# Router products on x times its scale, the root applied per token, router and memory-gate products in four column tiles

## What is computed

```python
def rmsnorm(x, g):
    y = x * lax.rsqrt(jnp.mean(x * x, axis=-1, keepdims=True) + EPS)
    return y * g

def latent_layer(x, mods, ...):
    sh1, sc1, g1, sh2, sc2, g2 = mods
    h = rmsnorm(x, ln1_g) * (1 + sc1) + sh1
    (cb, cc, ch), (nq, nk, nv), (mq, mk, mv), mo, ig, fg = project(h, w_in, ml_gate_b)
    ...
    x = x + g1 * merge(conv_o, na_o, ml_o, w_out)
    h2 = rmsnorm(x, ln2_g) * (1 + sc2) + sh2
    x = x + g2 * hier_moe(h2, w_rg, b_rg, w_re, b_re, w_gate, w_up, w_down)

def hier_moe(h, ...):
    gl = x @ w_rg + b_rg                  # 4 groups, x is h2
    el = (x @ w_re + b_re)                # 16 experts
    # best group, two best experts in it, softmax weights
    # expert: silu(x @ w_gate) * (x @ w_up), then @ w_down
```

## Time and profile before

| | |
|---|---|
| time, median of 3 runs | 1158.72 us (1154.29 to 1158.77) |
| profiled execution | 1159.24 us, span 1157.4 us |
| TensorE products (PE) | 1083.0 us busy, 94% |
| weight loads of TensorE (PEld) | 594.0 us, 51% |
| VectorE (DVE) | 396.9 us, 34% |
| ScalarE (ACT) | 246.0 us, 21% |
| GpSimd (POOL) | 56.5 us, 5% |
| mean granted clock of TensorE | 0.979 of full speed |
| read from HBM | 298.34 MB |

### The profile page before, as it was taken

How to read it: one execution, slowest core, us unless ns; L and a number is a source line. 1 busy time by engine, 2 the same in 40 slices (tenths; PEclk the granted TensorE clock), 3 DMA queues, 4 the chain that set the end, 5 groups by cost and what they waited for, 6 DMA issues and landing times.

```text
span 1157.4 us, 15554 instructions
## 1 busy us (share of the span) xinstructions
PE 1083.0 (94%) x6146; PEld 594.0 (51%) x6146; DVE 396.9 (34%) x1144; ACT 246.0 (21%) x517; POOL 56.5 (5%) x82
## 2 busy tenths in 40 slices
PE   3999999989999999999989999998898999999995
PEld 2546655676555445544334564566554644355443
DVE  3503033166282223222352301417627212222334
ACT  2210113152132111111141001415213211011113
POOL 1221000000002000000020000000000000000002
PEclk8999999999999999999999999999898999999998
DMA  8967562289618999999952445426450799999981
GB/s 312 362 169 217 192 219 84 74 312 308 271 36 311 401 412 412 413 413 413 405 201 73 146 155 211 153 74 255 128 217 2 294 360 413 412 398 406 414 353 55
DMA packets 92764, 302.59 MB, mean 261 GB/s; under 512 B 5789, under 2 KB 6161, under 8 KB 84369
## 3 DMA queue, kind: packets, MB, share of 16 engines
q1 hardware_dynamic: 89104, 293.84, 66.5%
q0 software_dynamic: 3584, 7.71, 2.8%
HBM read 298.34 MB, written 4.99 MB: 262 GB/s over the span
## 4 chain that ended last, share of the span: by engine, by line
PE 84%; DVE 6%; DMA 4%; ACT 2%; issue 2%; POOL 1%; SPq 0%; DVEq 0%; POOLq 0%; ACTq 0%
PE ps L1436 18%; PE ps L1005 17%; PE ps L1015 9%; PE ps L1492 9%; PE ps L1190 7%; PE ps L1257 5%; PE ps L959 4%; DMA ring<-in_w_up 3%; PE ps L1285 2%; PE ps L949 2%; PE ps L1287 2%; PE ps L1221 1%; PE ps L995 1%; PE ps L1155 1%; DMA ring<-in_w_mod 1%
## 5 line engine op out<-in xcount | busy, mean ns | idle before, releaser
L1005 PE MATMUL ps<-ring,hT 128*128 128x512 f32 (+1 forms) x480 | 194.9, 565 | 0.0
L1436 PE MATMUL ps<-ring,arena 128*64 128x512 f32 x608 | 174.4, 598 | 3.3 <-DMA ring<-in_w_up 3.3
L1005 PEld LDWEIGHTS ps<-ring,hT 128*128 128x128 f32 x480 | 90.5, 190 | 98.0 <-issue 94.7
L1436 PE MATMUL ps<-slot,arena 128*64 128x512 f32 x352 | 137.5, 601 | 2.0 <-issue 2.0
L2146 DVE SCALAR_TENSOR_TENSOR xT<-ps,modT,xT 128x128 f32<-128x128 f32 (+1 forms) x288 | 97.3, 409 | 69.4 <-PE ps L1190 60.2
L1015 PE MATMUL ps<-hT,ring 128*128 128x384 f32 x320 | 105.3, 487 | 0.0
L1436 PEld LDWEIGHTS ps<-ring,arena 128*64 128x64 f32 x608 | 54.9, 138 | 90.6 <-issue 90.6
L1190 PE MATMUL ps<-mixT,ring 128*128 128x384 f32 x256 | 85.1, 494 | 1.9 <-ACT mixT L1728 1.9
L1015 PEld LDWEIGHTS ps<-hT,ring 128*128 128x128 f32 x320 | 60.2, 190 | 41.5 <-issue 1.8
L2379 DVE TENSOR_TENSOR hT<-ps,arena 128x512 f32<-128x512 f32 x16 | 11.1, 692 | 203.6 <-PE ps L1436 203.6
L1492 PE MATMUL ps<-slot,arena 128*64 128x512 f32 x208 | 72.0, 597 | 0.0
(11 more groups left out here) (357 smaller groups left out, 1264.4 us busy)
## 6 DMA issues: line engine op xcount, KB each, us to landing
ring<-in_w_mod SPq DMA_DIRECT2D x24, 2048.0 KB, 12.5
ring<-in_w_gate SPq DMA_DIRECT2D x38, 1024.0 KB, 12.8
ring<-in_w_up SPq DMA_DIRECT2D x38, 1024.0 KB, 10.4
ring<-in_w_down SPq DMA_DIRECT2D x32, 1024.0 KB, 13.4
ring<-in_w_in SPq DMA_DIRECT2D x14, 2048.0 KB, 12.0
slot<-in_w_down SPq DMA_DIRECT2D x26, 1024.0 KB, 12.9
slot<-in_w_gate SPq DMA_DIRECT2D x22, 1024.0 KB, 11.4
slot<-in_w_up SPq DMA_DIRECT2D x22, 1024.0 KB, 10.6
```

What stands on the lines that cost most here:

```text
L1005: mm = pe.matmul(p[:, 0:n], hT[:, k, t * P:(t + 1) * P], w[:, k, c0:c0 + n], start=(k == 0), stop=(k == KT - 1))
L1436: mm = pe.matmul(out[which][64 * s:64 * s + 64, :], xg[:, k, cols[s]], w[i][:, k % 4, :], start=(k == 0), stop=(k == KT - 1))
```

## The change

**Router stage.** The router no longer works on normed tiles. With root r per token, gain a and shift b per feature, h2 = (x a) / r + b. ScalarE writes x a for tiles 0 to 6 into `hT` under the output products, VectorE for tile 7. TensorE multiplies these by `wroute`, now padded to 32 columns; tile k goes to column tile k mod 4 of the array, on partitions 32 (k mod 4) onward, so the eight products leave four partial sums (`parts`). Three products with a stacked identity add them and turn them to token order. The mean of squares is also made in token order (six products with one output column a tile, L1299), its root and reciprocal are three columns, `token_rstd`, and VectorE multiplies the logits by it and adds a bias that has the product of shift and router weights in it (`shift_bias`). That product comes from VectorE (two multiplications and a reduction) and one TensorE product, which stands ahead of the head transposes. For h2 the 24 transposes of x a stay open in PSUM, and six products of 512 columns add r b: the row of roots `std` times a diagonal of shifts that GpSimd builds (`shift_diag`). ScalarE and VectorE multiply by `token_rstd` as they drain h2. The squares move from `hT` to the space of `zqk`, and the banks of this stage are given one by one.

The core of the diff:

```diff
-    steps = [("gates",)]
-    steps += [("by_token", "mq", t) for t in range(3)] + [("by_token", "mk", t) for t in range(3)]
+    steps = [("gate_parts",), ("by_token", "mq", 0), ("gates",)]
+    steps += [("by_token", "mq", t) for t in (1, 2)] + [("by_token", "mk", t) for t in range(3)]
...
+                for j in range(2):
+                    pool.tensor_tensor(shift_diag[:, j], ident[:, None, :].broadcast_to((P, KT, P)),
+                                       modT[:, d, 24:32, j, None].broadcast_to((P, KT, P)), ALU.mult
+                                       ).then_inc(ly.shifts_ready, 1)
...
-                def gates():
+                def gate_sums():
                     pe.wait_ge(ly.wgp_ready, ly.number + 1)
-                    p = begin("gates")
+                    p = begin("gate_parts")
                     keep_busy(p, 5)
                     for k in range(KT):
                         wait_normed(0, k)
-                        mm = pe.matmul(p[:, 0:NT], wgp[:, k, :], hT[:, k, :], start=(k == 0), stop=(k == KT - 1))
-                    done(mm, "gates")
+                        lanes = slice(32 * (k % 4), 32 * (k % 4) + 32)
+                        mm = pe.matmul(p[lanes, 0:NT], wgp[:, k, :], hT[:, k, :], start=(k < 4), stop=(k >= 4))
+                    done(mm, "gate_parts")
+
+                def gates():
+                    bk.wait_drained(pe, "gate_parts")
+                    p = begin("gates")
+                    done(pe.matmul(p[:, 0:NT], cst[:, C_GATES:C_GATES + P], gate_parts, start=True, stop=True), "gates")
...
+                pe.wait_ge(ly.shift_sum_ready, ly.number + 1)
+                done(pe.matmul(begin("shift_logits")[:, 0:40], ones, shift_sum, start=True, stop=True), "shift_logits")
                 for h in range(4):
                     pe.wait_ge(ly.hnorm_ready, 4 * ly.number + h + 1)
...
-                sum_squares(1)
-                p = begin("lgT")
-                keep_busy(p, 5)
-                for k in range(KT):
-                    wait_normed(1, k)
-                    mm = pe.matmul(p[0:20, 0:NT], wroute[:, k, :], hT[:, k, :], start=(k == 0), stop=(k == KT - 1))
+                begin("lgT")
+                for k in range(4):
+                    route(k)
+                for k in range(4):
+                    turn_gained(k)
+                for k in range(4, KT):
+                    mm = route(k)
                 done(mm, "lgT")
+                sums = begin("sums")
+                for t in range(TILES):
+                    for k in (0, KT - 1):
+                        mm = pe.matmul(sums[:, t:t + 1], squares[1][:, k, t * P:(t + 1) * P], mean[:, 0:1],
+                                       start=(k == 0), stop=(k == KT - 1))
+                done(mm, "sums")
                 bk.wait_drained(pe, "lgT")
                 p = begin("lg")
                 for t in range(TILES):
-                    mm = pe.transpose(p[:, t * 20:(t + 1) * 20], lgT[:, t * P:(t + 1) * P], ident[0:20, 0:20])
+                    mm = pe.matmul(p[:, t * 20:(t + 1) * 20], parts[:, t * P:(t + 1) * P], cst[:, C_PARTS:C_PARTS + 20],
+                                   start=True, stop=True)
                 done(mm, "lg")
+                sum_squares(1)
+                for k in range(4, KT - 1):
+                    turn_gained(k)
+                turn_gained(KT - 1)
+                bk.wait_drained(pe, ("ss", 1))
+                pe.wait_ge(ly.shifts_ready, 2 * ly.number + 2)
                 for i in range(6):
-                    for n in range(4):
-                        mm = pe.transpose(p[:, n * P:(n + 1) * P], hT[:, upper * 4 + n, t * P:(t + 1) * P], ident)
+                    done(pe.matmul(ps[bk.bank(("h2", i))][:, :], std[:, t * P:(t + 1) * P],
+                                   shift_diag[:, 0 if t == 0 else 1, upper * 4:upper * 4 + 4, :].rearrange("p k n -> p (k n)"),
+                                   start=False, stop=True, skip_group_check=True), ("h2", i))
...
+                def gain():
+                    for k in range(KT):
+                        bk.wait_drained(act, ("wo", k))
+                        act.activation(squares[1][:, k, :], xT[:, k, :], ACT.Square).then_inc(ly.squares_ready, 1)
+                        if k < KT - 1:
+                            for j, cols in STREAMS:
+                                ins = act.activation(hT[:, k, cols], xT[:, k, cols], ACT.Copy, scale=gains[:, L, 1, k, j:j + 1])
+                            ins.then_inc(ly.gained_act, 1)
+                    p = full_of("lgT")
+                    drain("lgT", act.copy(parts, p[:, 0:NT]))
+                    p = full_of("sums")
+                    drain("sums", act.activation(token_root, p[:, 0:3], ACT.Sqrt, bias=eps))
+                    p = full_of(("ss", 1))
+                    drain(("ss", 1), act.activation(std[:], p[:, 0:NT], ACT.Sqrt, bias=eps))
...
+                for j in range(2):
+                    ins = dve.tensor_tensor(shift_route[:, j], wroute[:, :, 0:20], modT[:, L, 24:32, j, None].broadcast_to((P, KT, 20)),
+                                            ALU.mult)
+                link(ins)
+                dve.tensor_reduce(shift_sum.rearrange("p (j n) -> p j n", j=2), shift_route.rearrange("p j k n -> p j n k"),
+                                  AX.X, ALU.add).then_inc(ly.shift_sum_ready, 1)
...
-                drain("lg", dve.tensor_tensor(logits, p[:, 0:60].rearrange("p (t n) -> p t n", t=3),
-                                              rbias[:, None, :].broadcast_to((P, 3, 20)), ALU.add))
+                drain("lg", dve.tensor_tensor(logits, p[:, 0:60].rearrange("p (t n) -> p t n", t=3), wide(token_rstd, 20),
+                                              ALU.mult))
                 bk.wait_drained(dve, "lg")
+                link(dve.tensor_tensor(logits, logits, shift_bias, ALU.add))
```

More of the change, by code:

```diff
@@ L157, in constant_table @@
     t[:, C_JOB:C_JOB + OVERFLOW] = np.arange(OVERFLOW) + 0.5
+    for part in range(4):
+        for c in range(16):
+            t[32 * part + c, C_GATES + 32 * (c // 4) + c % 4] = 1.0
+    for part in range(4):
+        t[32 * part:32 * part + 20, C_PARTS:C_PARTS + 20] = np.eye(20)
     t[:, C_EPS] = EPS
@@ L226, in place_products @@
     for kind, *args in mixing_steps(layer):
-        if kind == "gates":
-            spread("gates")
+        if kind == "gate_parts":
+            spread("gate_parts")
+        elif kind == "gates":
+            spread("gates", over=before_heads)
         elif kind == "by_token":
@@ L263, in place_products @@
             bk.place(("C", *args), 7)
-    spread(*[("wo", m) for m in range(EARLY_OUT)], *[("hT", h) for h in range(4)],
-           *[("wo", m) for m in range(EARLY_OUT, 8)], ("ss", 1))
-    spread("lgT", "lg", *[("h2", i) for i in range(6)], "rank")
+    for m in range(EARLY_OUT):
+        bk.place(("wo", m), m)
+    bk.place("shift_logits", 5)
+    for h in range(4):
+        bk.place(("hT", h), HEAD_BANKS[h])
+    for m in range(EARLY_OUT, 8):
+        bk.place(("wo", m), m % 3)
+    bk.place("lgT", 7)
+    bk.place("sums", 1)
+    bk.place("lg", 7)
+    bk.place(("ss", 1), 5)
+    for i in range(6):
+        bk.place(("h2", i), H2_BANKS[i])
+    bk.place("rank", 5)
     for x in range(2):
@@ L607, in build @@
         loop_selw = sel[:, :, P:2 * P]
-        lgT = arena[0:20, 0:NT]
-        squares = (mixT, hT)
+        shift_diag = arena[:, 0:2048].rearrange("p (j k n) -> p j k n", j=2, k=KT)
+        shift_route = arena[:, 2048:2368].rearrange("p (j k n) -> p j k n", j=2, k=KT)
+        shift_sum = arena[:, 2368:2408]
+        shift_bias = arena[:, 2408:2468].rearrange("p (t n) -> p t n", t=3)
+        parts = arena[:, 2496:2496 + NT]
+        token_root = small[:, 48:51]
+        token_rstd = small[:, 52:55]
+        squares = (mixT, zqk[:].rearrange("p t d -> p (t d)").rearrange("p (k n) -> p k n", k=KT))
         xrow = ring[:, RING - 1, 0:3072].rearrange("p (t d) -> p t d", t=3)
@@ L976, in sum_squares @@
                     p = begin(("ss", n))
-                    if n == 1 or not ly.first:
-                        keep_busy(p, 2 if n == 1 else 4)
+                    if n == 0 and not ly.first:
+                        keep_busy(p, 4)
                     pe.wait_ge(ly.summed_ready, (n + 1) * (KT - 2))
@@ L1208, in _, with wait_gained, route, turn_gained @@
                     bk.wait_drained(pe, ("hT", h))
+                def wait_gained(k):
+                    if k < KT - 1:
+                        pe.wait_ge(ly.gained_act, ly.number * (KT - 1) + k + 1)
+                    else:
+                        pe.wait_ge(ly.gained_dve, ly.number + 1)
+                def route(k):
+                    wait_gained(k)
+                    lanes = slice(32 * (k % 4), 32 * (k % 4) + 32)
+                    return pe.matmul(ps[bk.bank("lgT")][lanes, 0:NT], wroute[:, k, :], hT[:, k, :], start=(k < 4),
+                                     stop=(k >= 4))
```

(27 more changed lines are left out.)

95 lines of the change are left out of this document (61 added, 34 removed).

## The result

The changed kernel takes 1149.58 us, the median of six runs (1147.39 to 1154.96), against 1158.63 for the kernel before in the same series. The ratio over all runs is 0.9933, with a 95% interval of 0.9907 to 0.9959; the two medians alone would give 0.9922. By the medians the gain is 9.05 us where 20.2 were forecast, and the time lies outside the range of 1132 to 1148. The profiled execution took 1154.96 us (span 1153.2, mean granted clock 0.975) and is the slowest of its six. The time goes with that clock: 1147.39 us came at 0.983. So I compare stages of the profiled executions, not their whole spans.

A forecast was written before the change was run, and what follows sets the result against it. TensorE bounds nearly everywhere, with engines waiting on each other in the router stage and experts living on their weight stream. 18.4 + 3.1 - 1.05 - 0.25 = 20.2 us off 1159.24 gives 1139.0, median 1138.6; range 1132 to 1148.

The forecast's parts named there:

- part 1: Router stage moved onto TensorE: 7.9 us won in layer 0 and 10.5 in layer 1, 18.4 us, if TensorE never waits.
- At most by half: VectorE's heads ahead of the output products: if GpSimd's diagonals disturbed them, their 3.24 us would grow by 1.6 us a layer.
- the filler's rows: Trace rows of six filler pieces in the router stage: 4.51 and 5.46 us after the clock fell, 2.6 at full clock.
- Router stage: From last output product to first expert product: 24.3 us in each layer, against 32.2 and 34.8 before.
- the rank row: Trace row of the router stage's rank products, 0.126 us a piece, used to price the one-column sum pieces at 1.5 us.
- Gates: Gate products on four column tiles side by side: 3.1 us won in layer 0, 0 in layer 1.
- New wait ahead of the heads: TensorE needs the shift sum before the head transposes: 0.8 us stall, -1.05 in all in layer 0; -0.25 in layer 1.
- Stream: Expert weight loads are not held and move with TensorE; the wait for the last weights stays near 19 us.
- The sign that I gave, 11 us earlier: Expert stage of layer 0: the wait for the last weights, still near 19 us, comes 11 us earlier.
- column tiles that do not overlap: Rival: 3.8 us more in each router stage and 3.8 in layer 0's gates, 1150 us; chance 0.04.
- The clock rival: Rival: clock falls earlier in the router stage, costing 2 to 3 us a layer, 1143 to 1149, say 1144; chance 0.13.
- the chance of 0.03 for a cost not seen: Whole kernel: an unforeseen cost leaves the time within 0.5% of the kernel before; chance 0.03.

The follow-up runs named there:

- experiment 1: The changed kernel, with GpSimd's two multiplications for the diagonals held until VectorE has made the shift sum; 1135.29 us, ratio 0.9802 against the kernel before.
- experiment 7: experiment 4 with the gate products of the kernel before the change, router stage as changed; 1139.83 us, ratio 0.9838 against the kernel before.
- experiment 4: experiment 1 with VectorE's shift sum made before its last heads and GpSimd starting behind the fourth head's norm; 1134.53 us, ratio 0.9785 against the kernel before.
- experiment 5: experiment 4 without the four filler pieces ahead of the ranks and with two instead of six behind them; 1130.55 us, ratio 0.9755 against the kernel before.

## Why the prediction was wrong

**The step that failed** is the one on the diagonals in part 1: "GpSimd builds the diagonals after its stores of the memory state, ahead of the 33.78 us of output products, which cover them; if they disturbed VectorE, the heads' 3.24 us would grow, at most by half, 1.6 us a layer." Three things in it are wrong.
- The work does not meet the heads' 3.24 us, it meets one of the three operations before them. I had asked where the result is used (far behind, after the output products), not what VectorE does when GpSimd starts. The trace of before has GpSimd's stores there, so the place could be read.
- It is a hold, not a slowing. "At most by half" was a guess without a row. The hold is 4.9 us (5.75 - 0.88), longer than the 3.77 us of the two GpSimd operations that the trace shows beside it.
- Its cost is not covered, because the new wait for the shift sum, which I priced at 1.05 us, puts the end of all VectorE work directly ahead of TensorE. TensorE's idle time of 5.6 us then costs clock. By the profiled executions of experiment 1 and the changed kernel the whole is 9.1 us in layer 0 and 8.2 in layer 1. By the medians it is 14.3 us for both layers; the changed kernel's profiled execution is 5.4 us above its median.

I should have carried it as a rival: GpSimd's work holds VectorE for its whole length. A price from this kernel's rows was to be had, since VectorE had 0.35 us to spare ahead of the heads in layer 0 and 2.4 in layer 1, and a fall of the clock costs 2 to 3 us by the filler's rows.

**The steps that held.**
- Router stage: 24.25 us in both layers against 24.3. The pieces fit one by one: 16 route pieces 1.56 (1.4), 24 transposes 2.77 (2.8), twelve one-column pieces 1.43 (1.5), twelve shift pieces 5.15 (5.1). Pricing the one-column pieces by the rank row was right: they took 0.12 us each.
- Gates: 2.9 us in layer 0 against 3.1; in layer 1 a loss of 0.4 by experiment 7 against 0.
- New wait ahead of the heads: 0.75 us idle in layer 0 (forecast 0.8) and none in layer 1, in experiment 1, where nothing holds VectorE. With the product it costs 11.3 - 10.1 = 1.2 us (forecast 1.05).
- Stream: the wait for the last weights of layer 0 is still 18.66 us long (18.92 before). It moved with TensorE, and no second round of experts ran. In the changed kernel it begins at 541.67, later than before (540.54); in experiment 1 at 530.92, 9.6 us earlier. The sign that I gave, 11 us earlier, did not follow from my own sum, which makes 7.9 + 3.1 - 1.05 = 9.95.
- Column tiles overlap, as the earlier trace rows said: eight route pieces of 384 columns take 0.78 us.

With the diagonals moved, the change is 1135.29 us where the sum said 1138.6. It is 3.3 us better than forecast, not exact. Where these come from is not shown, but single executions hold differences of that size: the profiled one of the kernel before lost 3.9 us in one round of its second layer's experts (15.65 and 1.99 us for what takes 13.73 in experiment 1; the clock was 0.76 and 0.81 from 994 to 1002), and 1.5 us at the first products behind the long weight wait of layer 0 (8.56 us for 32 pieces against 7.09, the clock 0.67 from 560 to 564).

**Of the rivals**, none was what happened. The measured 1149.58 us is nearly the time given for column tiles that do not overlap, 1150, but that is chance: they overlap. The clock rival is real, at 1.7 us in one layer of experiment 4 and as much in both of experiment 5, but in the changed kernel itself both router stages ran at the full clock. What the clock cost there, it cost in the output products, behind TensorE's idle time. Nearest to the truth was the chance of 0.03 for a cost not seen. It was too small for a change that puts new work on an idle engine, and its "within 0.5%" was not met either: the gain is 0.8% by the medians, 0.7% by the ratio.

## What to carry to other kernels

Work that goes to an idle engine is free only if the engine shares nothing with a busy one: look in the trace for what VectorE does at the moment when GpSimd's new instruction can start, not at when its result is used. Where both read SBUF, hold GpSimd back by one wait until VectorE is off the path; here that single line was worth 14.3 us. And a new wait on the critical engine should be priced with its producer late, since here 5.6 us of idle TensorE were paid twice, as the wait and as the half clock behind it.

## What the runs showed that I had not expected

- Beside two GpSimd multiplications of 128x1024 float32 (3.77 us) one VectorE operation of 0.35 us takes 5.22 us, so the two that follow each other on GpSimd hold it together. They take the same 3.76 us without VectorE beside them. The held operation starts at 271.44, 1.3 us before the first multiplication is recorded, and ends at 276.66, 0.15 us behind the second. So what the hold is longer than the multiplications lies ahead of their recorded start; whether they really begin earlier isn't settled, since the profile's spans on GpSimd are rough.
- Two GpSimd writes of the same size (1.86 us) held nothing, in either layer.
- The same narrow work in the same order kept the clock in one layer and lost it in the other, within one execution (experiment 4: 24.24 and 25.94 us).
- Between runs of one kernel the time follows the mean granted clock: the changed kernel's six go from 1147.39 us at 0.983 to 1154.96 at 0.975. The runs of the changed kernel spread over 7.6 us and those of experiment 1 over 9.8, so a smaller difference between the whole times of two profiled executions is no evidence on a change here.
